# Mixer's head distances from two rounded products, their tiles built by ScalarE

## What is computed

```python
acs = cumsum(dt * a_neg, axis=chunk)                 # per head, in chunks of 128 tokens
decay = exp(where(causal, acs[t] - acs[s], -inf))    # 128 x 128 for each head and chunk
y_intra = einsum(cb, decay, x * dt)
y_inter = einsum(cc, state) * exp(acs)
```

## Time and profile before

| | |
|---|---|
| median of 3 runs | 1630.81 us (1628.36 to 1634.38) |
| the profiled execution | 1634.04 us |
| its span | 1632.2 us |
| TensorE busy | 97% of the span |
| VectorE, ScalarE, GpSimd busy | 64%, 45%, 13% |

### The profile page before, as it was taken

The page is one execution under the profiler, slowest core; times in us unless marked ns, Lnnn a source line. Parts: engine busy times, 40 slices in busy tenths (PEclk is TensorE's granted clock), DMA queues, the critical chain, the costliest instruction groups (busy, mean ns, idle before and its releaser), DMA issues.

```text
span 1632.2 us, 24437 instructions
## 1 busy us (share of the span) xinstructions
PE 1588.8 (97%) x9794; PEld 1389.3 (85%) x9794; DVE 1047.6 (64%) x1284; ACT 730.7 (45%) x882; POOL 213.5 (13%) x182
## 2 busy tenths in 40 slices
PE   7999989999999999999999999899999999999997
PEld 6888788999999978888778887888999999788885
DVE  5554578888877545554665555888887765555545
ACT  6344344434445345444554344344444534544444
POOL 1000013353330000000000000244344100000000
PEclk9999989999999999999999999999999999999999
DMA  8655534465545555555555554345544465466551
GB/s 252 195 180 186 174 104 130 130 172 140 151 129 181 204 162 190 197 180 188 164 183 186 185 183 147 109 129 152 166 146 129 155 200 188 143 204 197 182 181 65
DMA packets 245073, 270.85 MB, mean 166 GB/s; under 512 B 12560, under 2 KB 226152, under 8 KB 245012
## 3 DMA queue, kind: packets, MB, share of 16 engines
q1 hardware_dynamic: 239504, 266.90, 52.2%
q10 hardware_dynamic: 5364, 2.98, 0.7%
q0 software_dynamic: 144, 0.15, 0.0%
HBM read 268.94 MB, written 1.05 MB: 165 GB/s over the span
## 4 chain that ended last, share of the span: by engine, by line
PE 87%; DVE 7%; issue 3%; ACT 2%; POOL 1%; DMA 1%; SPq 0%; ACTq 0%; POOLq 0%; DVEq 0%
PE bank L1353 28%; PE bank L1379 16%; PE bank L1381 16%; PE bank L1380 16%; DVE xcv L1024 2%; DVE w_lo L814 2%; PE bank L1534 1%; PE bank L1423 1%; PE bank L1737 1%; PE bank L1596 1%; PE bank L1540 1%; ACT w_hi L518 1%; DVE xcv L1021 1%; PE bank L1374 1%; PE bank L1367 1%
## 5 line engine op out<-in xcount | busy, mean ns | idle before, releaser
L814 DVE TENSOR_TENSOR w_lo<-w_raw,w_hi 128x2048 fp32r<-128x2048 f32 x251 | 587.7, 2344 | 291.8 <-ACT w_hi L518 291.8
L518 ACT ACTIVATE w_hi<-w_raw 128x2048 fp32r<-128x2048 f32 x251 | 478.9, 1912 | 219.9 <-PE bank L1381 114.3
L1353 PE MATMUL bank<-u_hi,w_hi 128*128 128x256 f32 x1152 | 338.2, 294 | 2.5 <-DVE u_lo L849 2.5
L1353 PE MATMUL bank<-u_lo,w_hi 128*128 128x256 f32 x1152 | 324.3, 281 | 0.0
L1353 PE MATMUL bank<-u_hi,w_lo 128*128 128x256 f32 x1152 | 324.0, 281 | 0.0
L1379 PE MATMUL bank<-w_hi,ha_hi 128*128 128x512 f32 x704 | 280.2, 398 | 3.8 <-DVE w_lo L814 2.9
L1381 PE MATMUL bank<-w_hi,ha_lo 128*128 128x512 f32 x704 | 275.2, 391 | 0.0
L1380 PE MATMUL bank<-w_lo,ha_hi 128*128 128x512 f32 x704 | 274.6, 390 | 0.0
L1353 PEld LDWEIGHTS bank<-u_hi,w_hi 128*128 128x128 f32 x1152 | 221.6, 192 | 9.4 <-issue 8.6
L1353 PEld LDWEIGHTS bank<-u_lo,w_hi 128*128 128x128 f32 x1152 | 221.4, 192 | 5.1 <-issue 4.8
L1353 PEld LDWEIGHTS bank<-u_hi,w_lo 128*128 128x128 f32 x1152 | 221.3, 192 | 0.0
(11 more groups left out here) (272 smaller groups left out, 2359.5 us busy)
## 6 DMA issues: line engine op xcount, KB each, us to landing
w_raw<-in_w_ffn_dram SPq DMA_DIRECT2D x262, 512.0 KB, 4.4
w_raw<-in_w_in_dram SPq DMA_DIRECT2D x160, 512.0 KB, 4.8
w_raw<-in_w_branch_b_dram SPq DMA_DIRECT2D x32, 512.0 KB, 4.2
w_raw<-in_w_branch_a_dram SPq DMA_DIRECT2D x16, 512.0 KB, 4.5
w_raw<-in_w_out_dram SPq DMA_DIRECT2D x16, 512.0 KB, 4.1
w_raw<-in_w_ple_gate_dram SPq DMA_DIRECT2D x16, 512.0 KB, 4.6
y_feat<-in_w_ple_dram ACTq DMA_DIRECT2D x2, 1024.0 KB, 5.0
h<-in_x_dram SPq DMA_DIRECT2D x2, 512.0 KB, 5.3
```

Of the source, the lines that this page charges most:

```text
L518: a_.activation(whi[slot][:, :, :], raw[slot][:, :, :], ACT.Copy).then_inc(sem["w_hi"], 1)
L814: v_.tensor_tensor(wlo[slot][:, :, :], raw[slot][:, :, :], whi[slot][:, :, :].bitcast(F32), ALU.subtract).then_inc(sem["w_lo"], 1)
L1353: i = mm(o, w[slot][:, k, cs], x[:, k, :], start=(k + q == 0 and not seeded), stop=(k == KD - 1 and q == 2 and not seeded), skip_group_che ...
```

## The change

dA is split by VectorE into `dA_hi` (rounded) and `dA_lo` (the rest) once a layer. R becomes `R_hi` and `R_lo`, both fp32r, two tiles of each; `tri_gt` and `ones` get fp32r copies. Each f32 matmul of `segments` and `from_start` becomes two fp32r matmuls that add up in the same bank. GpSimd builds no R any more. ScalarE does, one head (128x128) an instruction: 8 of them for a tile pair. Those of chunk 1 stand behind each half's exponentials of chunk 0 (`decay(0, b)`); those of chunk 0 of the next group stand at the end of a group, the hi part after the tanh of O and the lo part after the squares of y, which both stand ahead of the tanh of GA. In the later groups `step(2)` goes between the two halves of `decay(0)`, and `decay(1)` ahead of the second tanh. The row buffers of the gates move to another place in memory.

```diff
+                    def part_of(dst, part, g, c, half):
+                        for e in range(4):
+                            i = a_.activation(dst[half][:, e, :], tri_le[:, :], ACT.Copy,
+                                              scale=part[:, c, bass.ds(g * EH + (4 * half + e), 1)].bitcast(F32))
+                        return i
+
+                    def distances_of(g, c, half):
+                        part_of(R_hi, dA_hi, g, c, half)
+                        part_of(R_lo, dA_lo, g, c, half).then_inc(sem["r_built"], 1)
...
+                    def decay(c, b):
+                        act.wait_ge(sem["seg_done"], G * 6 + (2 * c + b + 1))
+                        a_.activation(seg[:, c, 4 * b:4 * b + 4, :],
+                                      bank[4 + 2 * c + b][:, :].rearrange("p (e t) -> p e t", e=4),
+                                      ACT.Exp).then_inc(sem["exp_done"], 1)
+                        if c == 0:
+                            distances_of(g, 1, b)
...
                     else:
-                        decay(0)
+                        decay(0, 0)
+                        step(2)
+                        decay(0, 1)
                         step(3)
+                        decay(1, 0)
+                        decay(1, 1)
                         tanh_conv(1, xcv[:, 0:2, :])
                         score_exp()
-                        decay(1)
                         step(4)
...
+                    if not last:
+                        act.wait_ge(sem["yi_done"], G + 1)
+                        act.wait_ge(sem["zth_ready"], G * 2 + 2)
+                        for half in range(2):
+                            part_of(R_hi, dA_hi, g + 1, 0, half)
                     act.wait_ge(sem["ha32_ready"], G + 1)
...
+                    if not last:
+                        act.wait_ge(sem["y_done"], G + 1)
+                        for half in range(2):
+                            part_of(R_lo, dA_lo, g + 1, 0, half).then_inc(sem["r_built"], 1)
                     scaled(GA)
...
+                dve.wait_ge(sem["dA_ready"], lay + 1)
+                ch.add(v_.tensor_copy(dA_hi[:, :, :], dA[:, :, :]))
+                ch.wait()
+                v_.tensor_tensor(dA_lo[:, :, :], dA[:, :, :], dA_hi[:, :, :].bitcast(F32), ALU.subtract)\
+                    .then_inc(sem["dA_split"], 1)
...
                         pe.wait_ge(sem["r_built"], G * 4 + (2 * c + half + 1))
-                        mm(bank[4 + 2 * c + half][:, :], tri_gt[:, :], R[half][:, :, :], start=True, stop=True)\
+                        mm(bank[4 + 2 * c + half][:, :], tri_gt_r[:, :], R_hi[half][:, :, :], start=True, stop=False)
+                        mm(bank[4 + 2 * c + half][:, :], tri_gt_r[:, :], R_lo[half][:, :, :], start=False, stop=True)\
                             .then_inc(sem["seg_done"], 1)
```

More of the change, by code:

```diff
@@ L111, in trunk @@
         g_fin = gate_a[:, 0:4, :].rearrange("p a b -> p (a b)")
+        top[0] = place(top[0], 64)
+        tri_gt_r = sb("tri_gt_r", [P, P], F32R)
+        ones_r = sb("ones_r", [P, P], F32R)
         ident = sb("ident", [P, P])
@@ L164, in trunk @@
         cth, a = at("cth", [P, 2, S], F32, a)
+        a = place(a, 64)
         late = a
+        xwe_at = late + NC * EH * HP * 4
         xw, a = at("xw", [P, NC, EH * HP], F32, a)
@@ L175, in trunk @@
         xin, a = at("xin", [P, 2, 2, S + 3], F32, a)
+        a = place(a, 64)
+        zth_at = a
         zth, a = at("zth", [P, 2, S], F32, a)
-        R = (xwe[:, :].rearrange("p (e t) -> p e t", e=4),
-             zth[:, :, :].rearrange("p a b -> p (a b)").rearrange("p (e t) -> p e t", e=4))
+        R_hi = [at(f"R_hi{b}", [P, 4, P], F32R, off)[0] for b, off in enumerate((xwe_at, zth_at))]
+        R_lo = [at(f"R_lo{b}", [P, 4, P], F32R, late + b * 4 * P * 4)[0] for b in range(2)]
         vtok, a = at("vtok", [P, NC, 258], F32, a)
@@ L206, in trunk @@
         row_one, a4 = at("row_one", [1, DEPTH, 104], F32, a4)
-        a5 = late
+        a5 = xcv_at
         r_i, a5 = at("r_i", [MH, S], F32, a5)
@@ L212, in trunk @@
         r_w, a5 = at("r_w", [MH, S], F32, a5)
+        assert a5 == xcv_at + 4 * S * 4
+        a5 = late + 4 * S * 4
         pre_row, a5 = at("pre_row", [40, S], F32, a5)
@@ L443, in token_columns @@
                     g_.tensor_copy(gtk[:, :].unsqueeze(2), tokc[:, :, bass.ds(g, 1)]).then_inc(sem["gtk_ready"], 1)
-                if first:
-                    pool.wait_ge(sem["dA_ready"], lay + 1)
-                    for half in range(2):
-                        distances_of(g, 0, half)
-                else:
-                    token_columns()
-                for half in range(2):
-                    pool.wait_ge(sem["seg_done"], G * 6 + (half + 1))
-                    distances_of(g, 1, half)
-                if first:
-                    token_columns()
+                token_columns()
                 pool.wait_ge(sem["p_exp"], G + 1)
@@ L470, in group @@
                 power(G + 1, "hvar_ready", hvar[:, :], "hrms_ready", hrms[:, :])
-                if not last:
-                    pool.wait_ge(sem["yi_done"], G + 1)
-                    pool.wait_ge(sem["zth_ready"], G * 2 + 2)
-                    for half in range(2):
-                        distances_of(g + 1, 0, half)
                 pool.wait_ge(sem["ysq_ready"], G + 1)
```

48 lines of the change are left out of this document (24 added, 24 removed).

## The result

| | before | after |
|---|---|---|
| median of the runs measured side by side | 1630.34 us (4 runs, 1628.36 to 1634.38) | 1662.78 us (4 runs, 1655.95 to 1666.52) |
| profiled execution | 1634.04 us | 1659.92 us |
| a later group of layer 0 / of layer 1 (mean of three) | 63.9 / 63.8 us | 68.3 / 69.8 us |

The changed kernel is slower: the ratio of the times is 1.0189, with a 95% interval of 1.0153 to 1.0225. The time of a group is here, and in all that follows, the distance from one VectorE read of unit O (`osg<-bank`) to the next.

What follows compares the result with a forecast made beforehand. TensorE, busy 97% of the span, was taken to bound the kernel. 1634.0 + 22.5 (later groups) + 0 (first groups) + 6 (clock) = 1662.5 us profiled, 1659 on the median's footing; range 1640 to 1677.

Steps and rivals of the forecast that it cites:

- The places and their order: Later groups: `segments` waits 12 times for ScalarE's heads, first tile behind the tanh, second behind V's copy and exponentials.
- The price of a head: ScalarE: one 128x128 head takes 0.30 us, ends 0.25 and 0.40; 256 heads, 77 us, mostly in idle time.
- The product: TensorE: a rounded pair takes 0.45 us against 0.86 for the f32 product, sparing 0.41 each, 19.7 us in all.
- The first stall: Later group, in X01: TensorE asks for chunk 1's first tile at 368.0, ready at 371.7, a 3.7 us wait.
- The second stall: Later group: TensorE asks for tile (1, 1) at 373.5, ready at 376.4, a 2.9 us wait.
- What comes back: Later group: four products' 1.64 us, then `from_start`'s two at 0.82 and its wait of 0.38, together 2.84.
- The net of a group: Later group: 6.6 us of stalls less 2.8 regained gives +3.8 us, 22.5 us over six groups.
- The clock: Later groups: lower clock falls behind one stall in three, 1 us a group, 6 us; ends 0 and 3 a group.
- The first groups: First group of each layer: TensorE's gain becomes a wait there, 0 us, ends -2.5 and +1 a layer.
- What it is spared is gained: Later groups: TensorE sets the end with no slack, busy 63.62 of 64 us, so spared time is gained.
- the first rival: TensorE finds its tiles and keeps the whole gain of 19.7 us and 2.3 of waits: 1609 us, chance 0.05.
- the second rival: The clock falls in every later group, 3 us each, 40 us with the stalls' 22.5: 1671 us, chance 0.2.

Runs made afterwards that it cites:

- the kernel with the filler: After, plus matmuls on zeros ahead of TensorE's two waits for chunk 1's tiles in the later groups, 15 and 10 of them: 1658.7 us.
- placement alone: After, but with before's f32 products kept and ScalarE building one tile of four heads wherever after builds a pair: 1634.9 us.
- after, lo tiles moved: After, with chunk 0's lo tiles in buffers free earlier, so ScalarE builds them ahead of `ha_hi` in the later groups: 1652.5 us.
- other order: After, but in the later groups ScalarE builds both tile pairs of chunk 1 in its idle time ahead of the first tanh: 1630.5 us.
- other order, lo tiles moved: Other order, with chunk 0's lo tiles in buffers free earlier, so ScalarE builds them ahead of `ha_hi` in the later groups: 1622.1 us.
- the fastest kernel: Other order, lo tiles moved, plus V's unit copy directly behind the first tanh, ahead of chunk 0's first exponentials, in the later groups: 1618.5 us.
- GpSimd's kernel with the wait of 3 us at `from_start`: Rounded products, with GpSimd building both tile parts where it built R in before, and ScalarE's list that of before: 1650.5 us.

## Why the prediction was right, and where not

The forecast was 1659 us and the time is 1662.8, inside the range. The mechanism, two stalls of TensorE behind ScalarE's heads, is the one predicted. That the sum came out so close is partly luck: against 1662.5 forecast for the profiled execution it took 1659.92, with later groups 31.4 us longer where 28.5 were forecast, and 5.5 us gained outside them where 0 was. Step by step:

**The places and their order: right.** `segments` waits 12 times, the first tile behind the tanh, the second behind V's copy and the exponentials. From the tanh's start to the first tile it was to be 3.5 us and is 3.5 (373.17 to 376.67).

**The price of a head: right.** 0.30 was taken, 0.29 measured, in 256 rows of 383 to 398 ns each.

**The product: nearly.** A pair takes 0.47, not 0.45 (in the kernel with the filler, its two matmuls and the first start behind them, 366.24 to 366.71), so 0.39 is spared, 2.3 us a group.

**The first stall: 3.7 predicted, 3.94 measured, 4.13 with the filler.** The copies ahead of the first tanh start later than I had them: measured from the last `outputs` matmul they are 1.7 us later than before, not 1.1. VectorE comes out of the stalled group 0.8 us behind TensorE (its read of O starts 0.5 after that matmul, where before it started 0.3 ahead of it), and y's squares with it. I had let only the lo part count. The convolution did come back, and GpSimd's columns did not collide with `w_lo`:

```profile
363.11 0.18 POOL L445 COPY ghn<-par 128x2 f32 x1
```

```profile
370.43 2.71 DVE L1047 SCALAR_TENSOR_TENSOR bcv<-xin,gcw,bcv 128x256 f32<-128x256 f32 x6
```

**The second stall: 2.9 predicted, 2.67 at full clock.** In after itself it is 1.05, because TensorE arrives late on the lower clock, which I had named ("would hide a part").

**What comes back: 2.84 predicted, 2.35 measured.** With the filler the stalls are 6.8 us and the group is 4.45 longer than before. That is 6 x 0.39 and nothing for the wait of 0.38 at `from_start`. The net of a group was to be 3.8 and is 4.45: this term was too small by 4 to 5 us in all.

Taking the stalls less what comes back is TensorE's account, and what sets the length shows better in VectorE's. Its timelines, before and after, from the scores' `pm` to unit Z0's `w_lo`:

```profile
373.14 0.61 DVE L1051 TENSOR_SCALAR pm<-bank,gtk 128x128 f32<-128x128 f32 x2 [0.56 <-PE bank L1556]
373.67 2.28 DVE L814 TENSOR_TENSOR w_lo<-w_raw,w_hi 128x2048 fp32r<-128x2048 f32 x1
```

```profile
383.01 0.61 DVE L1074 TENSOR_SCALAR pm<-bank,gtk 128x128 f32<-128x128 f32 x2 [2.27 <-PE bank L1583]
383.54 2.28 DVE L832 TENSOR_TENSOR w_lo<-w_raw,w_hi 128x2048 fp32r<-128x2048 f32 x1
```

Layer 0, group 2, cut at this `w_lo`:

| kernel | read of O to Z0's `w_lo`, us | from there to the next read of O, us |
|---|---|---|
| before | 27.99 | 36.03 |
| placement alone | 29.13 | 36.06 |
| after | 32.53 | 35.90 |
| filler on TensorE | 32.53 | 35.94 |
| after, lo tiles moved | 31.10 | 36.33 |
| other order | 27.84 | 35.92 |
| other order, lo tiles moved | 26.40 | 35.89 |
| the fastest kernel | 25.97 | 35.93 |

The second part hardly moves. The 36.33 is the one with the lower clock in it (35.91 in that kernel's group 3, at full clock); outside this table, GpSimd's kernel with the wait of 3 us at `from_start` has 36.6. In after, Z0's `w_lo` comes 4.5 us later than before, because the scores stand behind the second stall, and because Z0's unit copy stands behind both tile pairs (30.12 us after the read of O, 25.65 before); the whole loss of a group is there. What TensorE is spared behind that point, the two products and the wait of `from_start`, makes no group shorter in these rows: TensorE only comes to the next group 0.8 us further ahead of VectorE, and the next first stall is longer by that.

The prediction had seen that the copies of V and Z0 come 4 to 5 us later, and had counted nothing, since "VectorE's idle time ahead of Z0's read (2 us in this trace) takes the rest of the delay". It does not: that idle time went from 2.19 to 1.06 us, and from `cbm`, a little before it, to the next read of O it is 21.6 to 21.8 us in every kernel here. GpSimd's products on `seg` and `cs` (lines 460 and 464 of after, 11.5 us) run beside VectorE there; in the kernel with the other order `w_lo` takes 3.89 us beside them instead of 2.28. That GpSimd holds this stretch at its length is my reading; no run moved those products.

**The clock: 6 us predicted, 4 measured in the profiled execution,** none of it in layer 0. The step "it falls behind one stall in three" is wrong as told. It falls in all six later groups, and in layer 0 each time where the next wait hides it.

**The first groups: 0 predicted, about -5 in the profiled execution.** The six later groups are 31.4 us longer than before (28.5 predicted), the whole execution 25.9. Most of the other 5.5, 4.8, lies between layer 0's last group and layer 1's first (608.8 us against 613.6), in two places.

2.8 us are gained right behind layer 0's last group (from its read of O, 107.2 us before and 104.4 after to the same `w_lo`, at 580.93 and 592.23), where no tile is built. TensorE is at work all the time there at full clock in both kernels, but before it gets through fewer matmuls. Busy time by stretch, before and then after:

```profile
520.00:560.00 40.00, 40.00 (x338) 39.86 (x337) 23.43 (x21) 13.35 (x10) 0.00 (x0) 1.00 0.54 184
520.00:560.00 40.00, 40.00 (x345) 39.79 (x344) 25.26 (x23) 15.39 (x10) 0.00 (x0) 1.00 0.57 185
```

The ten other kernels take 104.4 to 105.3 us for that stretch. They share the moved buffers, the rounded constants and the split of dA, which the prediction put at nothing here; but of before there is one trace only, of a run 3.7 us above its median. Which of the two it is stays open.

The other 2.0 us are gained from that `w_lo` to O of layer 1's first group, and they aren't a trait of the change that can be relied on: over the same stretch the reordered kernel, whose first groups are after's to the letter, takes 3.4 us more than before. I didn't test either on its own.

**The premise under the rivals: wrong.** "What it is spared is gained" made the first rival 1609 us. The reordered kernel met its condition, a tile ready when TensorE comes, and ran in 1630. By the table above its group is shorter than before's by only 0.15 + 0.11 us, though TensorE has 2.3 us less to do in it. TensorE was busy 63.62 of 64 us, and I took the other engines' shares, 53 and 29 us, as room. The ring through both was not in the sum. In before VectorE waits for TensorE's scores for only 0.56 us (373.14, above), so it is nowhere far ahead. An estimate of the ring's length before, from rows: the fastest kernel's group of 61.9, plus what GpSimd's tiles added before, 0.64 in `w_lo` (2.92 against 2.28) and 0.77 in the first convolution (4.25 from 363.54 to 367.79 against 3.48): 63.3. So by this estimate TensorE had 0.7 us of a group to gain, not 2.3, until the ring was shortened too. For the forecast of after it made little difference, since the stalls were larger than both.

**The rule on the clock.** That the clock would be down behind the stalls was the second rival's ground (the Trainium skill, page "TensorE: Matmul & The Clock Gate", section "Why this matters for your kernels"). The trace agrees on the mechanism: 0.50 behind 3.9 us without matmuls, 1.00 with the filler in their place. The price that I had given that rival, 3 us a group, was too high: it was 0 in layer 0 and 1.4 in layer 1. What it costs goes by what stands behind TensorE at that moment.

## What to carry to other kernels

An engine that is busy 99% of a stage may be only just ahead of a ring of hand-overs between two others. Before counting what it is spared as gain, follow that ring once round and take its length; the sum of busy times does not give it. Cutting the period at one instruction of the second engine, in every kernel, shows which part of the ring a change moves and which it doesn't. Small work for an engine with idle time should go where the engine idles, and what keeps it from there is often only a buffer that is free too late: another place in memory was worth 8 us here, while the order of ScalarE's list was worth 32. And a move of work between engines is priced at what the receiving engine's neighbours wait for, not at its own rate: ScalarE's 4.7 us, where it idled, were free, and VectorE's 2.4 cost 2.3.

## What the runs showed of the hardware

- Filler matmuls on zeros kept the granted clock at 1.00 through waits of 4.1 and 2.7 us.
- Slow matmuls ahead of a wait that is longer than their delay cost nothing (layer 0 of after, 68.2 to 68.4 us a group; 68.2 to 68.5 with the filler and full clock).
- The same wait isn't always followed by the lower level: in the kernel "after, lo tiles moved" the granted clock went to 0.50 behind waits of 2.5 us in four later groups, and stayed at 1.00 in the two others.
- Two VectorE `tensor_scalar` of 128x256 took 1.57 us beside a GpSimd tile and 0.74 without it; six `scalar_tensor_tensor` took 4.15 and 2.71.
- GpSimd's copy of two columns took 0.18 us alone, and 2.26 beside VectorE's `w_lo`.
